# Leaving out the seven filler products of TensorE between the router's logits and the first token gather

## What is computed

```
def moe_swiglu(h, router, wg, wu, wd):
    ht = h.reshape(B * S, D)
    logits = jnp.einsum('td,de->te', ht, router).astype(jnp.float32)
    top_vals, top_idx = lax.top_k(logits, TOP_K)
    gates = jax.nn.softmax(top_vals, axis=-1)
    dense_gate = jnp.sum(jax.nn.one_hot(top_idx, N_EXPERTS) * gates[..., None], axis=1)
    out = jnp.zeros_like(ht)
    for e in range(N_EXPERTS):
        out = out + dense_gate[:, e:e + 1] * swiglu(ht, wg[e], wu[e], wd[e])
    return out.reshape(B, S, D)
```

## Time and profile before

| | |
|---|---|
| median of three runs | 1322.48 us (1320.91 to 1322.50) |
| profiled execution, its own time | 1325.81 us |
| its span, first to last instruction | 1323.9 us |
| mean granted clock of TensorE | 0.995 of full speed |
| TensorE matmul busy | 1277.3 us, 96% |
| TensorE weight load busy | 871.2 us, 66% |
| VectorE busy | 527.0 us, 40% |
| ScalarE busy | 378.0 us, 29% |
| GpSimd busy | 76.8 us, 6% |
| DMA | 396.16 MB, mean 299 GB/s |

### The profile page before, as it was taken

One profiled execution on the slowest core, in us unless ns is written; L12 is line 12 of the kernel. 1 busy time (PEld: TensorE's weight loads), 2 busy tenths in 40 slices (PEclk: granted clock), 3 DMA queues, 4 the chain that ended last, 5 costly groups with the idle time before them and its releaser, 6 DMA issues.

```text
span 1323.9 us, 30557 instructions
## 1 busy us (share of the span) xinstructions
PE 1277.3 (96%) x13811; PEld 871.2 (66%) x13811; DVE 527.0 (40%) x862; ACT 378.0 (29%) x506; POOL 76.8 (6%) x130
## 2 busy tenths in 40 slices
PE   8999999999999999978999999999998799999998
PEld 7879999889774454524445454454454488798896
DVE  6976545438964201102020020020202365747656
ACT  5565444325740000000000000000000347645643
POOL 3400000004400000000000000000001120000000
PEclk9999999999999999999999999999999999999999
DMA  9657765446499999999999999999999764243351
GB/s 308 208 182 251 240 239 196 143 127 192 141 379 410 409 377 426 422 426 424 425 425 422 425 424 424 424 424 424 424 410 425 304 226 157 96 128 128 99 193 60
DMA packets 88897, 396.16 MB, mean 299 GB/s; under 512 B 7043, under 2 KB 35315, under 8 KB 64194
## 3 DMA queue, kind: packets, MB, share of 16 engines
q1 hardware_dynamic: 81056, 381.31, 73.7%
q0 software_dynamic: 4832, 10.43, 2.5%
q10 hardware_dynamic: 2882, 2.50, 0.6%
HBM read 388.33 MB, written 8.65 MB: 300 GB/s over the span
## 4 chain that ended last, share of the span: by engine, by line
PE 76%; DVE 9%; DMA 9%; ACT 1%; SPq 1%; issue 1%; DVEq 0%; ACTq 0%
PE ps L2779 38%; PE ps L546 7%; PE ps L548 7%; PE ps L547 7%; DVE yT L2087 3%; DMA home_y<-in_moe_wd 3%; DMA home_x<-in_moe_wd 3%; DMA ering<-in_moe_wg 2%; PE ps L1253 2%; DVE low L536 2%; PE ps L1255 2%; PE ps L1254 2%; PE ps L2764 1%; SPq L508 1%; DMA gain_b<-in_norm_gain 1%
## 5 line engine op out<-in xcount | busy, mean ns | idle before, releaser
L2779 PE MATMUL ps<-ering,xe 128*32 128x384 f32 (+1 forms) x4064 | 307.7, 460 | 8.3 <-DMA ering<-in_moe_wu 6.1
L2779 PEld LDWEIGHTS ps<-ering,xe 128*32 128x32 f32 x4064 | 129.0, 110 | 181.3 <-issue 98.2
L536 DVE TENSOR_TENSOR low<-raw,high 128x2048 fp32r<-128x2048 f32 (+3 forms) x48 | 128.9, 2685 | 69.5 <-ACT high L531 67.1
L2266 DVE TENSOR_TENSOR eh<-eh,ps 128x384 f32<-128x384 f32 (+1 forms) x42 | 20.5, 487 | 326.6 <-PE ps L2779 326.6
L531 ACT ACTIVATE high<-raw 128x2048 fp32r<-128x2048 f32 (+3 forms) x47 | 105.5, 2245 | 94.7 <-PE ps L548 77.1
L546 PE MATMUL ps<-high,xT_hi 128*128 128x352 f32 (+1 forms) x368 | 128.3, 349 | 1.2 <-DVE xT_lo L2169 1.2
L548 PE MATMUL ps<-high,xT_lo 128*128 128x352 f32 (+1 forms) x368 | 127.2, 346 | 0.0
L547 PE MATMUL ps<-low,xT_hi 128*128 128x352 f32 (+1 forms) x368 | 126.9, 345 | 0.0
L2779 PE MATMUL ps<-ering,eT 128*32 128x256 f32 x1848 | 106.4, 384 | 8.0 <-DMA ering<-in_moe_wd 5.9
L2779 PEld LDWEIGHTS ps<-ering,eT 128*32 128x32 f32 x1848 | 60.6, 111 | 51.2 <-issue 10.1
L953 DVE TENSOR_TENSOR lowb<-rawb,highb 128x2048 fp32r<-128x2048 f32 x35 | 80.0, 2295 | 26.8 <-ACT highb L731 26.7
(11 more groups left out here) (462 smaller groups left out, 1982.5 us busy)
## 6 DMA issues: line engine op xcount, KB each, us to landing
ering<-in_moe_wu SPq DMA_DIRECT2D x49, 1408.0 KB, 27.1
ering<-in_moe_wg SPq DMA_DIRECT2D x48, 1408.0 KB, 27.5
ering<-in_moe_wd SPq DMA_DIRECT2D x24, 1536.0 KB, 31.0
rawb<-in_w_in SPq DMA_DIRECT2D x25, 1024.0 KB, 5.2
raw<-in_w_in SPq DMA_DIRECT2D x16, 1024.0 KB, 8.8
home_e<-in_moe_wd SPq DMA_DIRECT2D x8, 1536.0 KB, 29.0
home_f<-in_moe_wd SPq DMA_DIRECT2D x8, 1536.0 KB, 30.3
raw<-in_ffn_wg SPq DMA_DIRECT2D x8, 1408.0 KB, 6.1
```

Of the source, the lines that this page charges most:

```text
L536: nc.vector.tensor_tensor(low[:, c % SPLITS, 0:n], raw[:, c % RAWS, 0:n], f(high[:, c % SPLITS, 0:n]), ALU.subtract).then_inc(lo_made, 1)
L2779: mm = nc.tensor.matmul(out_of(rows), tokens, columns_of(s), start=begins, stop=ends, skip_group_check=True)
```

## The change

The two calls of `busy_filler` behind the router's logits are left out: four products between `logits_by_token` and the wait for `chosen_b`, and three between the count products and the wait for `pick`. The two calls ahead of the transposes stay. Nothing else is changed, on any engine.

```
             logits_by_token().then_inc(logits_ready, 1)
-            busy_filler(4)
             pe.wait_ge(route_landed, 32)
             pe.wait_ge(chosen_made, 1)
...
-            busy_filler(3)
 
             def gather(bank, t):
```

## The result

The change makes the kernel slower by a little: 1325.66 us, the median of 22 runs (1322.80 to 1328.23), against 1322.89 us for 22 runs of the kernel before on the same chip (1320.91 to 1325.90). The ratio is 1.0017, with an interval of 1.0012 to 1.0023, which is 2.3 us (1.6 to 3.0). The ratio is that of the means, 1325.51 and 1323.20 us; the medians lie 2.8 us apart. The change is within the 0.2% that I had called no change, but it is clear of the noise of that many runs, and the time lies above my range.

A forecast was written before the change was run, and what follows sets the result against it. TensorE's work was taken as the bound, on the chain for 76% of the span. 0.00 - 0.19 + 0.10 = -0.09 us from the runs' median gave 1322.4 us; range 1319.8 to 1325.0 us.

The forecast's parts named there:

- The first part: Four products behind the logits left out: hidden behind VectorE's chain, so 0.00 us saved; at most 1.16 us if uncovered.
- The second part: Three products behind the counts left out: the gather starts 0.19 us earlier, at 397.57 instead of 397.76 us.
- The gather's sum: Gather at the router: started 0.19 us earlier at half clock, its 48 records end at 401.60, a gain of 0.09 us.
- Passing on one to one: From router to kernel end: a shift of TensorE's first expert arrives in full, since loads follow the homes TensorE frees.
- absorption: Rival, experts' loads behind the router: DMA is full already, so nothing of the shift arrives; 1322.5 us, chance 0.12.
- what the missing activity costs: TensorE's clock at the router: one 3.41 us fall at its old place, no extra cost; bounds 0.18 slower, 1.10 us faster.
- my own signs of being right: At the router: first expert's product 0.0 to 0.3 us earlier, `chosen_b` at the same distance, one half-clock stretch of some 3.4 us.
- a rival of +3.2 us: Clock stays low two stretches more, through the gather into the first gate chunks; 1325.7 us, chance 0.05.
- one stretch more: Rival at the router: with TensorE idle, the clock stays low a second 3.41 us; +1.5 us, 1324.0 us, chance 0.18.

The follow-up runs named there:

- tiny fillers: Against the kernel before, the seven fillers stay in number and place, each cut to 16x32 by 16x8; ratio 1.0015 (1.0005 to 1.0024).
- seven and none: Against the kernel before, seven filler products instead of four in the first wait and none instead of three in the second; ratio 0.9997 (0.9989 to 1.0006).
- seven and three: Against the kernel before, seven filler products instead of four in the first wait, the second keeps its three; 1322.54 us, ratio 0.9989 (0.9980 to 0.9998).
- the eleven: Eleven more fillers between gather and first expert, added to the kernel with seven fillers in the first wait and three in the second; ratio to before 1.0012.
- dense fillers: Against the kernel before, the fillers of both waits replaced by eight and three bf16 products of 128x128 by 512 columns; ratio 0.9992 (0.9983 to 1.0001).

## Why the prediction was wrong

**The first part** was costed at 0.00 us since it hides behind VectorE. The reading is right: in after `chosen_b` comes at the same distance as before, and the fillers delayed nobody. Yet its two sets of runs without them are about 0.9 us slower, uncertain by 0.7, and in their traces the gather runs at half clock, wholly or in part (4.98 and 3.78 us instead of 2.80). **The second part** was costed at a gain of 0.19 us, of which 0.09 remain. That is right for an execution in which the clock falls in the midst of the fillers, as in my trace; in one where it doesn't, there is nothing to gain. The runs without this part are about 1.0 us slower, uncertain by 0.6.

**The gather's sum** held to the hundredth: for the trace of after the same working gives 398.37 + 2.88 at half clock + 1.15 = 402.40 us, and the record is at 402.39. **Passing on one to one** held, and absorption (0.12) fell.

**The step that failed** is "what the missing activity costs". I took the one fall in the trace of before as what every execution has, and concluded that the fillers don't hold the clock. So I put one fall of 3.41 us on both sides of the comparison and the term at nothing. The second trace of before has no fall, the three traces of the changed kernel have five stretches together, and over all runs the changed kernel has 4.5 us more at half clock. The missing term is at most half of that, 2.2 us of time. A hint stood in my own text: the profiled execution took 3.33 us more than the median "of which no stage of this trace is the cause". A stage can be part of the cause, the 3.41 us at half clock: against the floor it cost 1.5 us (7.22 - 5.72), nearly all of the 1.6 us by which the two traces' spans differ.

The first trace of the changed kernel met my own signs of being right, one stretch and a distance 0.09 us shorter. That was luck: the two other traces of the same kernel have two stretches and a distance about 1 us longer than the first trace of before. It was also inconsistent to write that no term could move the time by more than 2.6 us, with a rival of +3.2 us in the list.

Of the rivals, one stretch more (0.18, +1.5 us) is what happens in two of three traces, and it deserved the most weight. With less activity at the router the mean granted clock is lower, 0.9956 against 0.9973. The Trainium skill's page "TensorE: Matmul & The Clock Gate" (Part 1: The HAM clock gate) states that the low level is the default and that activity releases it; the runs agree. In the three traces of the changed kernel the clock falls 2.58, 1.24 and 2.18 us behind the end of line 2735. The same part of that page states that the monitor runs freely and isn't reset when a kernel starts; the traces agree so far. The point that I held against this rival, that TensorE was busy from 396.52 us on and the clock came back, was read from a kernel with fillers.

The range was too narrow for the same reason: both ends were built on that one execution. The 0.91 for a change within 0.2% came true at 0.17%, near the border and for another reason than the one given.

**Left open.** The traces alone give less than the runs: three distances of after average 7.84 us, two of before 6.47, 1.4 us apart, where the runs say 2.3. Five traces of a thing that differs by up to 1.5 us between traces of one kernel can't settle that. Nor is it known how often each kernel has no, one or two stretches at the router, since only the profiled executions show it.

## What to carry to other kernels

Work on TensorE that hides behind another engine's wait is not always free to remove: ask at what clock the next work on the critical path would run, and price a fall at half of its duration as far as it hits work. Never take the clock's course in one trace for the kernel's; compare the mean granted clock over many runs, and look at a second trace of the unchanged kernel before trusting a stretch that is a few us long. If fillers are used, let them cover the whole wait (with seven instead of four here, no trace has a fall), since with half-measures the fall can still come, and then they stand in the way at half clock.

## What the runs showed of the hardware

Where TensorE's clock fell at the router, in nine of fourteen traces, it stayed at half for 3.41 us (five traces) or 6.82 us (four). What TensorE did ahead of the gather, as two idle times, before and after the three small count products:

| kernel | idle, us | traces with a fall | distance, us |
|---|---|---|---|
| changed | 2.07 and 0.83 | 3 of 3 | 7.13 to 8.23 |
| first four left out | 2.07 and about 0.05 | 2 of 2 | 7.21 and 8.51 |
| tiny fillers | 1.72 and 0.41 | 1 of 1 | 8.01 |
| last three left out | 0.98 and 0.83 | 2 of 2 | 7.11 and 7.37 |
| before | 0.98 and about 0.05 | 1 of 2 | 5.72 and 7.22 |
| seven and none | 0.30 and 0.83 | 0 of 1 | 5.72 |
| seven and three | 0.31 and about 0.05 | 0 of 2 | 5.72, and 8.49 with the eleven |
| dense fillers | 0.16 and 0.23, then 0.16 | 0 of 1 | 5.73 |

At half clock the 48 records of the gather take 5.21 us instead of 2.80, and six records of fillers 1.63 us instead of 0.91.

The falls at the router seem to be a part of the spread of the runs. The standard deviation of the time is 1.3 to 1.5 us in the three sets of before (98 runs), and 0.7 to 0.9 us in the four kernels with the first wait covered (45 runs). They are not all of it: the end of line 2735, ahead of every change, differs by 3.1 us between the traces.
